# One gather tile padded to 128 rows, two buffers given up, and three w3 matrices fetched before the expert loop

## The reference, cut to what matters

```python
for l in range(DEPTH):                                   # DEPTH = 2
    ...
    h = layer_norm(DEEPNORM_ALPHA * h + mix, ln1_g[l], ln1_b[l])
    ffn = hier_moe(h, w_grp[l], b_grp[l], w_rtr[l], b_rtr[l], w1[l], w3[l], w2[l])
    h = layer_norm(DEEPNORM_ALPHA * h + ffn, ln2_g[l], ln2_b[l])

# hier_moe, for the tokens t and each expert e
hid = jax.nn.silu(jnp.einsum('td,edf->tef', t, w1)) * jnp.einsum('td,edf->tef', t, w3)
y = jnp.einsum('tef,efd->td', hid * combine[..., None].astype(hid.dtype), w2)
```

## Time and profile before

| | |
|---|---|
| median of 3 runs | 2472.61 us (2472.59 to 2474.36) |
| the profiled execution's own time | 2475.7 us |
| its span, first to last instruction | 2473.9 us |
| TensorE busy | 2269.3 us (92% of the span) |
| VectorE, ScalarE busy | 837.0 us (34%), 513.2 us (21%) |
| transfers | 426.67 MB, mean 172 GB/s |
| mean granted TensorE clock | 0.953 of full |

### The profile page before, as it was taken

One profiled execution on the slowest core, in us unless ns is written; L12 is line 12 of the kernel. 1 busy time (PEld: TensorE's weight loads), 2 busy tenths in 40 slices (PEclk: granted clock), 3 DMA queues, 4 the chain that ended last, 5 costly groups with the idle time before them and its releaser, 6 DMA issues. The chain is left out here.

```text
span 2473.9 us, 33836 instructions
## 1 busy us (share of the span) xinstructions
PE 2269.3 (92%) x12870; PEld 1724.1 (70%) x12870; DVE 837.0 (34%) x1877; ACT 513.2 (21%) x1174; POOL 53.9 (2%) x28
## 2 busy tenths in 40 slices
PE   8998899886999889988699999999999999999999
PEld 6766766543876766544575777888877677788887
DVE  3465233232456324223335333211122532321112
ACT  2213320002312331000333422010012243201000
POOL 0120000000021000000000000000000000000000
PEclk9889889998988998999899999999999999999999
DMA  7220249996321063999654134333345403343433
GB/s 228 80 87 35 103 170 378 425 425 240 113 87 44 35 272 146 419 425 420 224 136 145 35 137 136 137 137 136 136 159 137 145 34 137 102 140 135 168 136 119
DMA packets 165171, 426.67 MB, mean 172 GB/s; under 512 B 40409, under 2 KB 54294, under 8 KB 140454
## 3 DMA queue, kind: packets, MB, share of 16 engines
q1 hardware_dynamic: 165030, 424.80, 46.6%
HBM read 419.06 MB, written 1.05 MB: 170 GB/s over the span
## 5 line engine op out<-in xcount | busy, mean ns | idle before, releaser
L2061 PE MATMUL bank<-hT,W 128*128 128x256 f32 (+1 forms) x1440 | 329.5, 385 | 6.9 <-ACT b_gates L2189 5.9
L2061 PEld LDWEIGHTS bank<-hT,W 128*128 128x128 f32 (+1 forms) x1440 | 269.4, 190 | 53.0 <-issue 12.3
L261 PE MATMUL bank<-hT,W 128*128 128x272 f32 x928 | 247.6, 427 | 16.8 <-issue 11.7
L261 PEld LDWEIGHTS bank<-hT,W 128*128 128x128 f32 x928 | 191.3, 209 | 65.9 <-issue 23.3
L3038 PE MATMUL bank<-hT,W 128*128 128x256 f32 x1024 | 225.5, 381 | 6.7 <-DVEq L3095 6.7
L3054 PE MATMUL bank<-u_hid,W 128*128 128x256 f32 x1024 | 223.3, 379 | 0.0
L3038 PEld LDWEIGHTS bank<-hT,W 128*128 128x128 f32 x1024 | 195.6, 191 | 34.3 <-issue 7.4
L3054 PEld LDWEIGHTS bank<-u_hid,W 128*128 128x128 f32 x1024 | 194.6, 190 | 26.5
L1320 PE MATMUL bank<-e_sel,rowsH 128*128 128x128 f32 (+1 forms) x768 | 149.4, 328 | 0.0
L1434 PE MATMUL bank<-W,e_hs 128*32 128x256 f32 x1792 | 112.3, 409 | 32.3 <-DMA W<-in_w 29.8
L1320 PEld LDWEIGHTS bank<-e_sel,rowsH 128*128 128x128 f32 (+1 forms) x768 | 113.9, 204 | 37.2 <-issue 11.6
(11 more groups left out here) (555 smaller groups left out, 2784.4 us busy)
## 6 DMA issues: line engine op xcount, KB each, us to landing
W<-in_w SPq DMA_DIRECT2D x112, 1024.0 KB, 16.7
W<-in_w_in SPq DMA_DIRECT2D x41, 2048.0 KB, 8.1
e_Wd<-in_w SPq DMA_DIRECT2D x64, 1024.0 KB, 12.6
W<-in_w_up SPq DMA_DIRECT2D x16, 2048.0 KB, 8.4
W<-in_w_down SPq DMA_DIRECT2D x16, 2048.0 KB, 7.9
W<-in_w_out SPq DMA_DIRECT2D x8, 2048.0 KB, 8.2
e_w_ahead<-in_w SPq DMA_DIRECT2D x16, 1024.0 KB, 15.9
W<-in_mem_w_kv SPq DMA_DIRECT2D x6, 2048.0 KB, 10.3
```

Source lines behind the costliest of these rows:

```text
L261: mm = nc.tensor.matmul(bank[:, 0:T], w[:, k, c0:c0 + P], m.hT[:, k, :], **st)
L2061: mm = nc.tensor.matmul(o[0:n, 0:S2], w[:, k, a:a + n], m.hT[:, k, :], start=(k == 0), stop=(k == KT - 1))
```

## The change

It has four parts.

1. **Padding.** The plane of rowsH for the 16-token tile is set to zero on all 128 partitions by GpSimd at the start of `mix_and_route`; ScalarE waits for that (r_padded) before it copies rows. `gather` now takes all 128 partitions of all three planes, where it took 16 of the first.
2. **Sums in hT.** `experts` scales hT in place and adds the results there; yT is gone.
3. **Buffers given up.** Both layer norms use mixT as ln_sq. `select` works without e_eq: three tensor_scalar and three scalar_tensor_tensor of 128 columns in place of one operation of 768 and one of 384.
4. **w3 early.** With W3_AHEAD = 3, SyncE fetches w3 of three of the four experts of group 1 in `mix_and_route`, behind w1 of group 1. One goes into xT (unused there), two into new buffers. In `experts` only the fourth is fetched.

```diff
@@ mix_and_route
-        m.ln_sq = sb("ln_sq", [P, KT, T])
+        m.ln_sq = m.mixT
...
                             sp.dma_start(m.w1_ahead[:, j, :], expert_weights(A, l, BLOCKS_GROUP + j)[0]).then_inc(S["e_w1_ahead"], 16)
+                        for j in range(W3_AHEAD):
+                            sp.dma_start(m.w3_ahead[j], expert_weights(A, l, BLOCKS_GROUP + j)[1]).then_inc(S["e_w3_ahead"], 16)
...
+                nc.gpsimd.memset(m.rowsH[:, 0, :], 0.0)
+                pool.drain().then_inc(S["r_padded"], 1)
...
+                act.wait_ge(S["r_padded"], 1)
@@ gather
-        for c, (t0, nt) in enumerate(TILES):
-            mm = nc.tensor.matmul(o, m.rowsH[0:nt, c, d * P:(d + 1) * P], m.sel[0:nt, c, :], start=(c == 0), stop=(c == 2))
+        for c in range(3):
+            mm = nc.tensor.matmul(o, m.rowsH[:, c, d * P:(d + 1) * P], m.sel[:, c, :], start=(c == 0), stop=(c == 2))
@@ experts
-                w3(fixed, 1)
+                w3(fixed, 1, first=W3_AHEAD)
...
-                            pe.wait_ge(S["e_w3_in"], g * 64 + 64)
+                            pe.wait_ge(S["e_w3_in"], 64 if isinstance(g, int) and g == 0 else g * 64 + (64 - 16 * W3_AHEAD))
+                            if ahead3:
+                                pe.wait_ge(S["e_w3_ahead"], 16 * W3_AHEAD)
...
-                    nc.vector.tensor_tensor(eq[:, :, :, :], m.slot_of[:, :, :].unsqueeze(3).to_broadcast([P, 3, 2, P]),
-                                            m.count[:, :].unsqueeze(1).unsqueeze(1).to_broadcast([P, 3, 2, P]), ALU.is_equal)
+                    for c in range(3):
+                        nc.vector.tensor_scalar(sel[:, c, :], m.count[:, :], m.slot_of[:, c, 0:1], None, ALU.is_equal)
                     dve.drain()
-                    nc.vector.tensor_tensor(sel[:, :, :], eq[:, :, 0, :], eq[:, :, 1, :], ALU.add)
+                    for c in range(3):
+                        nc.vector.scalar_tensor_tensor(sel[:, c, :], m.count[:, :], m.slot_of[:, c, 1:2], sel[:, c, :], ALU.is_equal, ALU.add)
+                    dve.drain()
...
-                        nc.vector.tensor_tensor(m.yT[:, d, :], m.yT[:, d, :], ps[6 + d % 2][:, 0:T], ALU.add).then_inc(S["e_y_free"], 1)
+                        nc.vector.tensor_tensor(m.hT[:, d, :], m.hT[:, d, :], ps[6 + d % 2][:, 0:T], ALU.add).then_inc(S["e_y_free"], 1)
...
-                nc.vector.tensor_scalar(m.yT[:, :, :], m.hT[:, :, :], ALPHA, None, ALU.mult)
+                nc.vector.tensor_scalar(m.hT[:, :, :], m.hT[:, :, :], ALPHA, None, ALU.mult)
```

More of the change, by code:

```diff
@@ L30 @@
 LEAST_GROUPS = 4
+W3_AHEAD = 3
 ALPHA = (2.0 * DEPTH) ** 0.25
@@ L1339, in experts @@
         Wd = m.Wd
-        eq = sb("e_eq", [P, 3, 2, P])
         sel = m.sel
@@ L1351, in experts @@
         m.rstd = used_up[:, KT * T:KT * T + T]
-        m.ln_sq = sb("ln2_sq", [P, KT, T])
+        m.ln_sq = m.mixT
         early = m.ln_sq[:, :, :].rearrange("p k t -> p (k t)")
@@ L1374, in w1, with w3 @@
                         sp.dma_start(m.W[:, j, 0:KT * DE], expert_weights(A, l, ids[j])[0]).then_inc(S["e_w1_in"], 16)
-                def w3(ids, i):
+                def w3(ids, i, first=0):
                     sp.wait_ge(S["e_w3_done"], i)
-                    for j in range(G):
+                    for j in range(first, G):
                         sp.dma_start(m.W[:, j, KT * DE:2 * KT * DE], expert_weights(A, l, ids[j])[1]).then_inc(S["e_w3_in"], 16)
@@ L1420, in scatter, with up @@
                         nc.tensor.matmul(ps[6 + d % 2][:, 0:T], y[:, d * P:(d + 1) * P], back[:, 0, :], start=True, stop=True).then_inc(S["e_part"], 1)
-                def up(g, arrived, ahead=False):
+                def up(g, arrived, ahead=False, ahead3=False):
                     for h in range(2):
@@ L1429, in up @@
                         else:
-                            pe.wait_ge(S["e_w3_in"], g * 64 + 64)
+                            pe.wait_ge(S["e_w3_in"], 64 if isinstance(g, int) and g == 0 else g * 64 + (64 - 16 * W3_AHEAD))
+                            if ahead3:
+                                pe.wait_ge(S["e_w3_ahead"], 16 * W3_AHEAD)
                         for k in range(KT):
                             for j in range(G):
-                                weights = m.w1_ahead[:, j, k * DE:(k + 1) * DE] if x == 0 and ahead else Wu[:, j, x, k, :]
+                                weights = Wu[:, j, x, k, :]
+                                if x == 0 and ahead:
+                                    weights = m.w1_ahead[:, j, k * DE:(k + 1) * DE]
+                                elif x == 1 and ahead3 and j < W3_AHEAD:
+                                    weights = m.w3_ahead[j][:, k * DE:(k + 1) * DE]
                                 mm = nc.tensor.matmul(ps[2 + x][32 * j:32 * j + 32, DE * x:DE * x + DE], hs[:, k, 32 * j:32 * j + 32], weights,
@@ L1470, in _ @@
                 between(0)
-                up(1, 64, ahead=True)
+                up(1, 64, ahead=True, ahead3=True)
                 between(1)
@@ L1621, in _ @@
                     dve.wait_ge(S["e_part"], (n + 2) * KT + (d + 1))
-                    nc.vector.tensor_tensor(m.hT[:, d, :], m.yT[:, d, :], ps[6 + d % 2][:, 0:T], ALU.add).then_inc(S["e_y_free"], 1)
+                    nc.vector.tensor_tensor(m.hT[:, d, :], m.hT[:, d, :], ps[6 + d % 2][:, 0:T], ALU.add).then_inc(S["e_y_free"], 1)
                     dve.drain().then_inc(S["n2_ready"], 1)
@@ L1632 @@
 s_idx s_rel s_acc s_logit s_logit_sb s_max s_exp s_den s_prob s_pT s_pT_sb s_pv s_out
-o_mm o_added n1_centred n1_mean n1_squares n1_var n1_rstd n1_scaled n1_done r_logitT r_logitT_sb r_logit r_exp_in r_exp r_masks r_rows r_rows_sb r_counts r_ranks r_nb r_starts r_ended r_spread r_token_row r_table
-e_w1_ahead e_w1_in e_w3_in e_down_in
+o_mm o_added n1_centred n1_mean n1_squares n1_var n1_rstd n1_scaled n1_done r_logitT r_logitT_sb r_logit r_exp_in r_exp r_masks r_rows r_rows_sb r_counts r_ranks r_nb r_starts r_ended r_spread r_token_row r_table r_padded
+e_w1_ahead e_w3_ahead e_w1_in e_w3_in e_down_in
 e_sel e_gather0 e_gather1 e_hs0 e_hs1 e_w1_done e_w3_done e_sil e_hid e_turn e_hidT e_down e_y e_y_free e_back e_part n2_ready n2_centred n2_mean n2_squares n2_var n2_rstd n2_scaled n2_done""".split()
@@ L1741, in lsb @@
                         return lay.enter_context(nc.sbuf_tensor(name, shape, F32))
-                    m.yT = lsb("yT", [P, KT, T])
                     m.rowsH = lsb("rowsH", [P, 3, D])
@@ L1752, in first_block @@
                     m.w1_ahead = lsb("e_w1_ahead", [P, BLOCKS_GROUP, KT * DE])
+                    m.w3_ahead = [m.xT[:, :, :].rearrange("p k t -> p (k t)")] + [lsb(f"e_w3_ahead{j}", [P, KT * DE])[:, :] for j in range(1, W3_AHEAD)]
                     m.sel = lsb("e_sel", [P, 3, P])
```

## The result

The change takes 2449.24 us in the median of 4 runs (2445.55 to 2453.43), against 2472.6 us before (2469.65 to 2474.36, 4 runs). The ratio is 0.9907, with a 95% interval of 0.9885 to 0.9929: 0.9% faster.

A forecast was written before the change was run, and what follows sets the result against it. TensorE was taken to set the pace before T0, the weight transfers after. Two layers of -12.1 us (7.5 + 1.6 + 3.0) and +2.6 for the tail make -21.6: 2472.6 to 2451 us, range 2443 to 2462.

The forecast's parts named there:

- The gather at full clock: Gather of group 1, padded: 48 products in 5.35 us in place of 8.35, -3.0 us a layer.
- The gather of group 0: First gather, at low clock: padded, 7.8 us in place of 15.3 with the clock rising after 4.5 us, -7.5 us.
- `up(0)`: Products of up for group 0, then at full clock: 7.0 us in place of 8.65, -1.6 us a layer.
- Rival B: The clock stays low through the first gather; T0 gains 4.6 + 3.0 us, total 2460 us; chance 0.14.
- T0: End of down(0), when SyncE issues w2 of group 1, 396.1 us in layer one; forecast 12.1 us earlier per layer.
- Two regimes: TensorE sets the pace before T0, transfers after; the 171.5 us from there to the last w3 wait stay.
- w3 early: Three w3 transfers of group 1 moved ahead: the same bytes are left after T0, so worth 0.
- The tail: Products of up on the last w3, slowed by a falling clock: +0.6 and +2.0 us by layer, +2.6 us together.
- The bounds of the small terms: New select at 0.9 to 3.6 us, hidden; GpSimd's clearing of the plane up to 6 us, normally costing 0.
- Rival D: The change of rows is not what slows the gather; nothing before T0 moves, 2472.6 us; chance 0.10.
- E: Slower: the clock stays low after each longer TensorE wait, 2590 us if wholly low; chance 0.04.

The follow-up runs named there:

- Padded late: The change with the padding only in the gathers of group 2 and later: 2466.08 us, ratio 0.9983 to the kernel before.
- padded early: The change with the padding only in the gathers of groups 0 and 1: 2449.12 us, ratio 0.991 to the kernel before.
- the kernel with w2 early and the old order: The change, fetching w2 of three group 1 experts early instead of w3, with w3 of group 2 still issued before w1 of group 3: 2442.51 us.

## Why the prediction was right

It said 2451 us; the median is 2449.24. Step by step, against the profiled execution:

- **The gather at full clock.** -3.0 us forecast, 3.0 measured (8.35 to 5.36 us), and for its reason. At a change of height the loading of weights pauses, where otherwise a load starts every 0.11 us, and with half the changes about half of the 3.0 us goes (1.35).
- **The gather of group 0.** -7.5 forecast. From its start to `up(0)` it took 16.55 us before (365.87 less 349.32) and 8.57 and 10.0 after, -8.0 and -6.5. The clock rose 2.8 and 6.0 us after the start, where I took 4.5 as the middle of 3.3 and 5.9. Both lie just outside these two, and that their mean is near 4.5 is luck: in the other kernels with these gathers padded, the time from the start to `up(0)` was 7.2 to 10.1 us. Rival B is out: the clock rose inside the gather in both layers.
- **`up(0)`.** -1.6 forecast, 8.65 to 7.04 us measured.
- **T0.** 12.1 us earlier by the sum. The first gather to T0 fell from 46.8 us to 34.2 and 35.7, so 12.5 us in layer one and 11.1 in layer two.
- **Two regimes.** T0 to the last wait was to stay. It was 171.5 and 172.8 us before, and 171.7 and 171.6 after. Padded late and padded early show it from both sides. It was 171.4 to 173.0 us in all kernels that leave the same bytes at T0. Within that scatter layer two gained 1.2 us that I had not forecast, about as much as its T0 fell short.
- **w3 early.** Worth 0 forecast; 0.1 and 1.2 us in the comparison with padding alone, no more than that scatter.
- **The tail.** +0.6 and +2.0 forecast, +1.0 (5.12 to 6.13 us) and +1.7 (3.66 to 5.35) measured. The clock fell, as I said, but the idle time before the last products was 5.7 and 4.8 us and not 7.8. In layer one `up` on the w3 before it took 5.58 us (at 526.06) at the low clock, where it had taken 3.66 (at 537.94), and that used up 1.9 of the 2.9 us that the gather behind it gave.
- **What I missed.** The longer waits for w2, 3.6 and 4.7 us in layer one: I had put all of the new waiting on w3, at 6 to 8 us a wait, and the longest wait for W was 6.3. TensorE reaches `down` before w2 lands, since w2 is queued with the rest. These waits cost nothing, since T0 to the last wait did not grow. And the time outside the stage: I took it as fixed, and it moves by 9 us with the clock. The medians average over part of that, the profiled pair does not.
- **The bounds of the small terms.** The new `select` takes 1.65 us in the trace (362.18 to 363.83) where the old one took 1.6 (369.80 to 371.4), inside the bounds of 0.9 and 3.6. My lower bound came from an operation of one column, and one of 128 took 0.28 or 0.35 us. Clearing the plane took 0.95 us and not 6, at 291 us, long before ScalarE needs it.
- **Rival D** fell with the length of the gather in every padded kernel. **E** was not seen: from the first gather to the last wait no low stretch of the change's clock lasts over 6.9 us.

What stays open: the norms' shared scratch and the sums in hT were not tried one by one. Padding alone and the whole change agree within their scatter, so no sign of either is left.

## What to carry to other kernels

First find the moment from which the transfers run without a hole. Here TensorE's work set the time before it and only the bytes did behind it, and the same edit was worth all or nothing. A buffer that comes free should take those weights whose turn comes after that moment, and the order of the issues has to be checked for the hole that this opens. And where TensorE sets the pace and a contraction mixes a short tile with full ones, try to pad it to full height, or to put the short products side by side. This was measured with fp32 products of 128 columns only.

## What the hardware did that I had not expected

- The step in the height of a product lies between 64 and 96 rows: 8.36 us a gather with 64, 5.46 with 96.
- The clock around the first gather is not fixed. In the kernel with w2 early and the old order it did not fall around the first gather of layer one, and the gather, with the small product inside it, ended within these 7 us at PEclk 1.00:

```profile
346.00:353.00 7.00, 6.70 (x57) 6.04 (x56) 3.15 (x20) 0.00 (x0) 0.00 (x0) 1.00 0.00 0
```

  That is 1.3 us less than the change had there (7.24 us from its start to `up(0)`, against 8.57).
- The stretch between the two stages, with the same work for TensorE, took from 321.6 to 331.4 us in the profiles here, in step with the granted clock: 321.6 and 321.7 us at 0.95, 324.5 to 325.0 at 0.94, 327.7 at 0.93, and 330.3 to 331.4 at 0.92. These 9.8 us are half of the spread of the runs (2459.27 to 2478.86 us for the kernel before, at a granted clock of 0.960 and 0.952 over the whole run), and more than one of this change's terms.
